# Strassen pairs of the last up projection: the first product is copied between banks by ScalarE and added onto by TensorE, in a new order of the seven products

## The chip, the cores and the metric

One core of one Trainium2 chip. The metric is device time in microseconds, the median of several executions.

## What is computed

Two blocks of a transformer follow each other on a sequence of 512 tokens with 1024 features: sparse attention, a convolutional feed-forward, a state-space mixer, a second feed-forward, and then a block with a short convolution and the gated feed-forward of which the change touches the up projection:

```python
def swiglu(h, w_gate_up, w_down):
    g, u = jnp.split(h @ w_gate_up, 2, axis=-1)
    return (jax.nn.silu(g) * u) @ w_down
...
h = modulate(rms_norm_2(x, norm_gains[i, 2]), sh_f, sc_f)
h = swiglu(h, ffn_w_gate_up[i], ffn_w_down[i])
x = x + g_f[:, None, :] * rms_norm_2(h, norm_gains[i, 3])
```

`w_gate_up` is 1024 x 5632: 22 tiles of 128 gate features and 22 of 128 value ("rise") features. Everything is float32.

## The kernel before, in words

Activations lie with features on the 128 partitions and the 512 tokens along the free dimension, in two halves, HEAD (tokens 0 to 255) and TAIL (256 to 511). Every float32 product is made from three matmuls in a reduced format: each operand is split into a high part (a ScalarE copy to `fp32r`) and a low part (VectorE: the operand less its high part), and TensorE adds hi x hi, hi x lo and lo x hi in a PSUM bank. Weights come in panels of 128 x 1024 by DMAs of SyncE's queue into `raw` buffers (three, and from the pairs on a fourth, `raw_more`); ScalarE writes `whi`, VectorE writes `wlo`, in four slots.

The last up projection, `UP3`, has 44 panels, gate and value tiles alternating. The first 8 (`CLASSIC`) are multiplied in the ordinary way, 24 matmuls of 512 tokens each. The other 36 form 18 pairs (`PAIRS`), one gate and one value tile, and each pair is one step of Strassen's scheme in Winograd's form: the weights of the pair are a 2 x 2 matrix of blocks (A11, A12 the two halves of the gate tile's 1024 inputs, A21, A22 those of the value tile), the activations another, and seven products of 12 matmuls of 256 tokens take the place of eight. The weight sums of the scheme, S1 to S4, are made by GpSimd for each pair in four 512-wide operations (`wsum`, lines 877 to 884); the activation sums (`t_hi`, `t_lo`) are made once.

The weights of a pair are five *units*, each with a high part (`unit_hi`, line 2019) and a low part (`unit_lo`, line 2861): A11 (for P1), S21 (1024 wide, P6 and P5), A12 (P2), S34 (1024 wide, P7 and P3), A22 (P4). A unit's slot is free when the last product that uses it is done; `s_ulo` counts the low parts made, and every product waits for its unit.

Nothing is scheduled automatically. Each engine's order is written by hand: `pairs_up3` for TensorE, one loop over pairs n for ScalarE, one for VectorE, one for GpSimd, and semaphores join them. TensorE takes P1, P6, P5, P7, P2, P4, P3 of pair n and then goes to pair n+1. There are three banks to a pair, X, Y and Z, in two sets that alternate. X gets P1 and then P2 on top (gate head). Y gets P6, P7 and P4 on top of each other, Z gets P5 and P3. ScalarE copies P1 out of X into `first_p` (line 2064), and five VectorE sums of 256 tokens (`part`, line 2874) put the results together, each from a bank and an SBUF tensor:

```python
P(1): part_u[0] = Y(P6) + first_p
P(2): part_u[1] = Y(P6+P7) + first_p
P(3): rise tail = Z(P5) + part_u[1]
P(4): rise head = Y(P6+P7+P4) + first_p
P(5): c12 (gate tail) = Z(P5+P3) + part_u[0]
```

(the five calls of `part`, abridged). Each reads a bank onto which TensorE's next product waits to be added: `s_part` counts them. ScalarE applies silu to the head (from X, line 2038) and the tail (from `c12`, line 2041), and VectorE multiplies all 512 tokens at once (`pair_hidden`, line 2880). VectorE runs, for each n: c12 of pair n-1, low part of S34(n), hidden product of n-1, P(1), low parts of A22(n) and A11(n+1), P(2), P(3), low parts of S21(n+1) and A12(n+1), P(4). In pairs 1 to 4 and in the last one the hidden tiles are split into parts for the down projection as well (`hidden_hi`, line 2030; `hidden_lo`, line 2867), which write over operands no longer in use. The down projection `DOWN3` follows with its panels in three parts.

## Time and profile before

| | us |
|---|---|
| median of 3 runs | 2101.13 |
| lowest, highest | 2096.67, 2101.19 |
| the profiled execution | 2104.0 |
| its span | 2102.3 |
| TensorE busy in it | 2055.5 |
| VectorE busy | 1389.3 |
| ScalarE busy | 906.7 |
| GpSimd busy | 254.7 |

The profiled execution is one run, 2.9 us above the median; its span is shorter than its time by what lies around the program. Busy times include overlap of an instruction's end with the next one's start, so that a full engine shows 100% whatever the spacing of its matmuls; the count of matmuls in a stretch tells more.

### The profile page before, as it was taken

To read this page: it belongs to the slowest core of one execution; us is meant where nothing else is said; L and a number is where in the kernel's file an instruction comes from. 1 tells how busy PE (TensorE), PEld (TensorE's weight loads), DVE (VectorE), ACT (ScalarE), POOL (GpSimd) and SP (SyncE) were. 2 spreads that over 40 slices of the span, in tenths; PEclk is the share of its full clock that TensorE was granted. 3 is DMA by queue.
4 is the path that set the end of the run, shared out by engine and by line. 5 is a ranking of instruction groups with operands and counts; after the bars stand their busy time and mean duration, and the time that the engine had idled before them with its cause. 6 is when DMAs were issued, how large, how long until landed. Compare 5 with 4: busy or idle time off the path is not lost.

```text
span 2102.3 us, 30885 instructions
## 1 busy us (share of the span) xinstructions
PE 2055.5 (98%) x12072; PEld 1737.5 (83%) x12072; DVE 1389.3 (66%) x2383; ACT 906.7 (43%) x1641; POOL 254.7 (12%) x227
## 2 busy tenths in 40 slices
PE   8999999999999999998899999999999999999998
PEld 6877779888888988787789888888898898999887
DVE  5378847877755588537864877766465457888624
ACT  4267754534331354438742543432241234444521
POOL 0000002000000110004601100000020013565101
PEclk9999999999999999999899999999999999999999
DMA  8110002332246323335422232236422322233331
GB/s 276 61 41 22 21 12 81 111 100 91 90 157 233 111 81 104 100 103 164 138 81 81 86 105 100 91 113 234 145 91 91 101 71 73 99 103 109 111 90 61
DMA packets 69696, 217.04 MB, mean 103 GB/s; under 512 B 8112, under 2 KB 11568, under 8 KB 69296
## 3 DMA queue, kind: packets, MB, share of 16 engines
q1 hardware_dynamic: 67536, 208.72, 30.2%
q10 hardware_dynamic: 2016, 6.36, 0.9%
q8 instruction: 96, 1.57, 0.3%
q14 instruction: 48, 0.39, 0.1%
HBM read 211.70 MB, written 2.23 MB: 102 GB/s over the span
## 4 chain that ended last, share of the span: by engine, by line
PE 86%; DVE 8%; ACT 2%; issue 2%; DMA 1%; POOL 1%; SPq 0%; ACTq 0%; DVEq 0%
PE bank L951 23%; PE bank L953 23%; PE bank L952 23%; PE bank L972 3%; PE bank L974 2%; PE bank L973 2%; PE bank L1299 1%; DVE pbuf L2412 1%; PE bank L1276 1%; PE bank L894 1%; DVE pbuf L2431 1%; PE bank L1198 1%; PE bank L1253 1%; POOL h L826 1%; PE bank L925 1%
## 5 line engine op out<-in xcount | busy, mean ns | idle before, releaser
L951 PE MATMUL bank<-xhi,whi 128*128 128x512 f32 (+1 forms) x1624 | 615.6, 379 | 14.9 <-DVE xlo L2124 8.2
L953 PE MATMUL bank<-xhi,wlo 128*128 128x512 f32 (+1 forms) x1624 | 607.5, 374 | 0.0
L952 PE MATMUL bank<-xlo,whi 128*128 128x512 f32 (+1 forms) x1544 | 579.5, 375 | 0.0
L1560 ACT ACTIVATE whi<-raw 128x1024 fp32r<-128x1024 f32 (+1 forms) x283 | 293.0, 1037 | 617.8 <-PE bank L953 592.8
L2110 DVE TENSOR_TENSOR wlo<-raw,whi 128x1024 fp32r<-128x1024 f32 (+1 forms) x283 | 341.5, 1207 | 260.8 <-ACT whi L1560 260.2
L951 PEld LDWEIGHTS bank<-xhi,whi 128*128 128x128 f32 x1624 | 306.9, 189 | 78.6 <-issue 13.0
L953 PEld LDWEIGHTS bank<-xhi,wlo 128*128 128x128 f32 x1624 | 306.8, 189 | 58.1
L952 PEld LDWEIGHTS bank<-xlo,whi 128*128 128x128 f32 x1544 | 292.2, 189 | 53.8
L826 POOL TENSOR_TENSOR h<-tmp,h 128x256 f32<-128x256 f32 x92 | 82.6, 919 | 1475.6 <-DVE tmp L2135 1471.3
L951 PE MATMUL bank<-hid_hi,whi 128*128 128x512 f32 (+1 forms) x416 | 151.3, 364 | 0.0
L953 PE MATMUL bank<-hid_hi,wlo 128*128 128x512 f32 (+1 forms) x416 | 149.8, 360 | 0.0
L952 PE MATMUL bank<-hid_lo,whi 128*128 128x512 f32 (+1 forms) x416 | 149.7, 360 | 0.0
L2278 DVE TENSOR_TENSOR upad<-bank,rstd_b 128x512 f32<-128x512 f32 x88 | 60.6, 690 | 72.7 <-PE bank L953 67.4
L953 PEld LDWEIGHTS bank<-hid_hi,wlo 128*128 128x128 f32 x416 | 78.4, 188 | 12.6
L951 PEld LDWEIGHTS bank<-hid_hi,whi 128*128 128x128 f32 x416 | 78.5, 189 | 12.4
L952 PEld LDWEIGHTS bank<-hid_lo,whi 128*128 128x128 f32 x416 | 78.4, 189 | 12.4
L972 PE MATMUL bank<-t_hi,whi 128*128 128x256 f32 x288 | 82.7, 287 | 2.2 <-DVE part_u L2874 2.1
L1648 ACT ACTIVATE tmp<-upad,par 128x512 f32<-128x512 f32 x88 | 70.6, 805 | 31.8 <-DVE upad L2278 31.8
L974 PE MATMUL bank<-t_hi,wlo 128*128 128x256 f32 x288 | 81.3, 282 | 0.0
L973 PE MATMUL bank<-t_lo,whi 128*128 128x256 f32 x288 | 81.3, 282 | 0.0
L1749 ACT ACTIVATE pbuf<-pbuf,stat 128x512 f32<-128x512 f32 (+3 forms) x128 | 70.3, 552 | 15.9 <-DVE stat L2415 15.9
L952 PE MATMUL bank<-hid_l,whi 128*128 128x512 f32 (+1 forms) x208 | 74.9, 360 | 0.0
(340 smaller groups left out, 3675.2 us busy)
## 6 DMA issues: line engine op xcount, KB each, us to landing
raw<-w SPq DMA_DIRECT2D x286, 512.0 KB, 3.3
ada_w<-w_ada SPq DMA_DIRECT2D x64, 384.0 KB, 4.1
raw<-w SPq DMA_DIRECT2D x24, 384.0 KB, 3.3
row<-cum_rows SPq DMA_DIRECT2D x32, 256.0 KB, 3.6
xbuf<-exp_rows SPq DMA_DIRECT2D x24, 256.0 KB, 3.6
raw_more<-w SPq DMA_DIRECT2D x9, 512.0 KB, 3.2
w_k<-w_cmp ACTq DMA_DIRECT2D x1, 2048.0 KB, 11.4
w_v<-w_cmp ACTq DMA_DIRECT2D x1, 2048.0 KB, 7.7
```

Source lines behind the costliest of these rows:

```text
L826: pool.tensor_tensor(h[:, j, hs], tmp[:, j % 2, hs], h[:, j, hs], ALU.add).then_inc(s_h, 1)
L951: pe.matmul(bk[:, tok], whi[w][:, cols], x_hi, start=k == 0, stop=False, skip_group_check=split)
L952: pe.matmul(bk[:, tok], whi[w][:, cols], x_lo, start=False, stop=False, skip_group_check=split)
L953: return pe.matmul(bk[:, tok], wlo[w][:, cols], x_hi, start=False, stop=last, skip_group_check=split)
L972: pe.matmul(to, whi[w][:, cols], x_hi, start=begins and kb == 0, stop=False, skip_group_check=True)
L973: pe.matmul(to, whi[w][:, cols], x_lo, start=False, stop=False, skip_group_check=True)
L974: mm = pe.matmul(to, wlo[w][:, cols], x_hi, start=False, stop=ends and kb == 3, skip_group_check=True)
L1560: act.activation(whi[g % SLOTS][:, 0:n], raw[RAW_OF[g]][:, 0:n], ACT.Copy).then_inc(s_hi, 1)
L1648: act.activation(tmp[:, c % 2, :], upad[:, c % 2, 2:2 + S], ACT.Identity, scale=col("ffn_w", 3 * k + 2), bias=col("ffn_b", k)).then_inc(s_ ...
L1749: act.activation(pbuf[:, s % 3, g, 0:n], pbuf[:, s % 3, g, 0:n], ACT.Exp, scale=QSCALE, bias=stat[:, b, 4 + g:5 + g], accum_out=stat[:, b, ...
L2110: dve.tensor_tensor(wlo[g % SLOTS][:, 0:n], raw[RAW_OF[g]][:, 0:n], whi[g % SLOTS][:, 0:n].bitcast(F32), ALU.subtract).then_inc(s_lo, 1)
L2278: dve.tensor_tensor(upad[:, c % 2, 2:2 + S], in_bank(c)[:, :], rstd_b[:, :], ALU.mult)\
```

## The change

Bank Y now starts from P1. ScalarE copies bank X to bank Y (`seed`), and TensorE adds P6, P7 and P4 onto it. So Y holds in turn U2 = P1 + P6, U3 = U2 + P7 and the value tile's head, U3 + P4. ScalarE keeps U2 and U3 in SBUF (`keep_u2`, `keep_u3`), VectorE makes the gate tail from Z and U2 (`gate_tail`), the rise tail from Z and U3 (`corner_tail`), and the hidden tile in two halves: the head directly from bank Y (`hidden_head`), the tail from SBUF (`hidden_tail`). TensorE's order is P1(0), and then for each n P5, P6, P2, P7, P1(n+1), P4, P3. The hidden tiles split during the pairs are so in pairs 4 to 7, not 1 to 4. GpSimd's code moves into a function and keeps its order. Helpers get the phase's name as an argument; lines that change for this alone, and the buffers for split hidden tiles that follow the new last uses, are left out here.

```diff
-ORDER_P = ("P1", "P6", "P5", "P7", "P2", "P4", "P3")
-UNIT_LAST = {"A11": "P1", "S21": "P5", "A12": "P2", "S34": "P3", "A22": "P4"}
+UNIT_LAST = {"A11": "P1", "S21": "P6", "A12": "P2", "S34": "P3", "A22": "P4"}
...
+def products_of(name):
+    order = [(0, "P1")]
+    for n in range(PAIRS[name]):
+        order += [(n, p) for p in ("P5", "P6", "P2", "P7")]
+        order += [(n + 1, "P1")] if n + 1 < PAIRS[name] else []
+        order += [(n, "P4"), (n, "P3")]
+    return order
...
             def pairs_up3():
-                for n in range(PAIRS):
-                    if n < 2:
-                        pe.wait_ge(s_ev, EV["UP3"] + (6, 8)[n])
-                    else:
-                        pe.wait_ge(s_sg, SG3 + CLASSIC // 2 + 2 * (n - 2) + 1)
-                    pair_product(n, "P1", "X")
-                    if n >= 2:
-                        pe.wait_ge(s_part, 5 * (n - 2) + 4)
-                    pair_product(n, "P6", "Y")
-                    if n >= 2:
-                        pe.wait_ge(s_part, 5 * (n - 2) + 5)
-                    pair_product(n, "P5", "Z")
-                    pe.wait_ge(s_part, 5 * n + 1)
-                    pair_product(n, "P7", "Y")
-                    pe.wait_ge(s_p1, n + 1)
-                    pair_product(n, "P2", "X")
-                    pe.wait_ge(s_part, 5 * n + 2)
-                    pair_product(n, "P4", "Y")
-                    pe.wait_ge(s_part, 5 * n + 3)
-                    pair_product(n, "P3", "Z")
+                first(0)
+                for n in range(PAIRS["UP3"]):
+                    if n >= 2:
+                        pe.wait_ge(s_c12, pair_made("UP3", n - 2))
+                    pair_product("UP3", n, "P5", "Z")
+                    pe.wait_ge(s_seed, pair_made("UP3", n))
+                    pair_product("UP3", n, "P6", "Y")
+                    pair_product("UP3", n, "P2", "X")
+                    pe.wait_ge(s_u2, pair_made("UP3", n))
+                    pair_product("UP3", n, "P7", "Y")
+                    if n + 1 < PAIRS["UP3"]:
+                        first(n + 1)
+                    pe.wait_ge(s_u3, pair_made("UP3", n))
+                    pair_product("UP3", n, "P4", "Y")
+                    pe.wait_ge(s_c22, pair_made("UP3", n))
+                    pair_product("UP3", n, "P3", "Z")
...
+            def seed(n):
+                act.wait_ge(s_prod, PRODUCT["UP3", n, "P1"])
+                if n < 2:
+                    act.wait_ge(s_ev, EV["UP3"] + (6, 8)[n])
+                else:
+                    act.wait_ge(s_hh, pair_made("UP3", n - 2))
+                act.activation(half_of(pair_bank(n, "Y")), half_of(pair_bank(n, "X")), ACT.Copy).then_inc(s_seed, 1)
+            def keep_u2(n):
+                act.wait_ge(s_prod, PRODUCT["UP3", n, "P6"])
...
+                act.activation(u2[:, n % 2, :], half_of(pair_bank(n, "Y")), ACT.Copy).then_inc(s_u2, 1)
+            def keep_u3(n):
+                act.wait_ge(s_prod, PRODUCT["UP3", n, "P7"])
...
+                act.activation(u3[:, :], half_of(pair_bank(n, "Y")), ACT.Copy).then_inc(s_u3, 1)
...
-            for n in range(PAIRS):
-                unit_hi(n, "S34")
+            seed(0)
+            for n in range(PAIRS["UP3"]):
+                unit_hi("UP3", n, "S34")
                 if n:
                     pair_silu(n - 1, TAIL)
-                act.wait_ge(s_prod, product_done(n, "P1"))
-                if n >= 2:
-                    act.wait_ge(s_part, 5 * (n - 2) + 4)
-                act.activation(first_p[:, n % 2, :], half_of(pair_bank(n, "X")), ACT.Copy).then_inc(s_p1, 1)
-                unit_hi(n, "A22")
-                unit_hi(n + 1, "A11")
-                unit_hi(n + 1, "S21")
-                if 1 <= n < 5:
-                    hidden_hi(n - 1)
-                if n == PAIRS - 1:
+                unit_hi("UP3", n, "A22")
+                unit_hi("UP3", n + 1, "A11")
+                keep_u2(n)
+                unit_hi("UP3", n + 1, "S21")
+                pair_silu(n, HEAD)
+                unit_hi("UP3", n + 1, "A12")
+                if 4 <= n < 8:
+                    hidden_hi(n - 4)
+                if n == PAIRS["UP3"] - 1:
                     for k in range(4, 8):
                         hidden_hi(k)
-                unit_hi(n + 1, "A12")
-                pair_silu(n, HEAD)
+                keep_u3(n)
+                if n + 1 < PAIRS["UP3"]:
+                    seed(n + 1)
...
-            for n in range(PAIRS):
+            for n in range(PAIRS["UP3"]):
                 if n:
-                    part(n - 1, 5, c12[:, :], "Z", "P3", part_u[:, 0, :])
-                unit_lo(n, "S34")
+                    gate_tail(n - 1)
+                unit_lo("UP3", n, "S34")
                 if n:
-                    pair_hidden(n - 1)
-                dve.wait_ge(s_p1, n + 1)
-                part(n, 1, part_u[:, 0, :], "Y", "P6", first_p[:, n % 2, :])
-                unit_lo(n, "A22")
-                unit_lo(n + 1, "A11")
-                if 1 <= n < 5:
-                    hidden_lo(n - 1)
-                part(n, 2, part_u[:, 1, :], "Y", "P7", first_p[:, n % 2, :])
-                dve.wait_ge(s_part, 5 * n + 2)
-                part(n, 3, rise[:, cols_of(TAIL)], "Z", "P5", part_u[:, 1, :])
-                unit_lo(n + 1, "S21")
-                unit_lo(n + 1, "A12")
-                if n == PAIRS - 1:
+                    hidden_tail(n - 1)
+                unit_lo("UP3", n, "A22")
+                unit_lo("UP3", n + 1, "A11")
+                if 4 <= n < 8:
+                    hidden_lo(n - 4)
+                unit_lo("UP3", n + 1, "S21")
+                unit_lo("UP3", n + 1, "A12")
+                if n == PAIRS["UP3"] - 1:
                     for k in range(4, 7):
                         hidden_lo(k)
-                    weight_lo(START["DOWN3"])
-                part(n, 4, rise[:, cols_of(HEAD)], "Y", "P4", first_p[:, n % 2, :])
+                corner_tail(n)
+                hidden_head(n)
+            weight_lo(START["DOWN3"])
             hidden_lo(7)
```

How the orders of two engines read at the same point, a pair of the steady state. On VectorE, before, from `c12` of one pair to the A11 part of the next but one (`wlo_57` is S34's slot, `wlo_58` that of A22, `wlo_59` that of A11 and A12):

```order
L2874 TENSOR_TENSOR c_205<-bank,part_u 128x256 [waits pair_products_made]
L2861 TENSOR_TENSOR wlo_57<-wsum,whi_53 128x1024 [waits pair_units_hi_made]
L2880 TENSOR_TENSOR hid_f_170<-tmp 128x512 [waits pair_parts_added,gates_silu]
L2874 TENSOR_TENSOR part_u<-bank,first_p 128x256 [waits pair_products_made,first_products_kept]
L2861 TENSOR_TENSOR wlo_58<-raw_52,whi_54 128x512 [waits pair_units_hi_made]
L2861 TENSOR_TENSOR wlo_59<-raw_50,whi_55 128x512 [waits pair_units_hi_made]
```

and after the change:

```order
L2931 TENSOR_TENSOR c_205<-bank,u_203 128x256 [waits gates_silu,pair_products_made]
L2917 TENSOR_TENSOR wlo_57<-wsum,whi_53 128x1024 [waits pair_units_hi_made]
L2951 TENSOR_TENSOR hid_f_170<-tmp 128x256 [waits corner_tails_added,gates_silu]
L2917 TENSOR_TENSOR wlo_58<-raw_52,whi_54 128x512 [waits pair_units_hi_made]
L2917 TENSOR_TENSOR wlo_59<-raw_50,whi_55 128x512 [waits pair_units_hi_made]
```

The units keep their order; the hidden product is half as wide, and the sum between it and A22 is gone. On TensorE, before, where P1 (`whi_55`, `wlo_59`) begins, it follows P3 of the pair ahead:

```order
L972 MATMUL bank<-xhi,whi_53 128x256
L973 MATMUL bank<-xlo,whi_53 128x256
L974 MATMUL bank<-xhi,wlo_57 128x256
L972 MATMUL bank<-xhi,whi_55 128x256 [waits pair_units_lo_made,gates_silu]
L973 MATMUL bank<-xlo,whi_55 128x256
L974 MATMUL bank<-xhi,wlo_59 128x256
```

and now it follows P7 (which reads `t_hi`, `t_lo`) of it:

```order
L996 MATMUL bank<-t_hi,whi_53 128x256
L998 MATMUL bank<-t_lo,whi_53 128x256
L999 MATMUL bank<-t_hi,wlo_57 128x256
L996 MATMUL bank<-xhi,whi_55 128x256 [waits pair_units_lo_made,gates_silu]
L998 MATMUL bank<-xlo,whi_55 128x256
L999 MATMUL bank<-xhi,wlo_59 128x256
```

P1 of the next pair has moved ahead of P4 and P3 of this one, with its wait for the unit's low part. On ScalarE, after the change, from S34's high part on:

```order
L2048 ACTIVATE whi_53<-wsum 128x1024 [waits pair_products_made,weight_sums_made]
L2074 ACTIVATE tmp<-c_205 128x256 [waits hidden_made,gate_tails_added]
L2048 ACTIVATE whi_54<-raw_more 128x512 [waits pair_products_made,raw_landed3]
L2048 ACTIVATE whi_55<-raw_51 128x512 [waits pair_products_made,raw_landed1]
L2090 ACTIVATE u_203<-bank 128x256 [waits gate_tails_added,pair_products_made]
L2048 ACTIVATE whi_56<-wsum 128x1024 [waits pair_products_made,weight_sums_made]
L2070 ACTIVATE tmp<-bank 128x256 [waits hidden_heads_made,pair_products_made]
L2048 ACTIVATE whi_55<-raw_51 128x512 [waits pair_products_made,raw_landed1]
L2097 ACTIVATE u_204<-bank 128x256 [waits corner_tails_added,pair_products_made]
L2083 ACTIVATE bank<-bank 128x256 [waits hidden_heads_made,pair_products_made]
```

In the place of one copy (`first_p`, before A22's high part) stand three: U2 ahead of S21's high part, U3 and the seed of the next pair at the end.

## Rows read from the trace of the kernel before

**Rows 1.** The page, busy time, share of the span and count of instructions

```profile
PE 2055.5 (98%) x12072; PEld 1737.5 (83%) x12072; DVE 1389.3 (66%) x2383; ACT 906.7 (43%) x1641; POOL 254.7 (12%) x227
```

**Rows 2.** Windows of the pair stage: length, busy of PE, PEld, DVE, ACT, POOL, PEclk, DMA

```profile
1800.00:1840.00 40.00, 38.13 (x314) 37.31 (x313) 34.23 (x45) 19.49 (x33) 23.89 (x16) 1.00 0.27 93
1840.00:1965.00 125.00, 125.00 (x1038) 124.19 (x1037) 105.64 (x138) 59.40 (x102) 69.60 (x45) 1.00 0.31 101
```

**Rows 3.** Waits of PE, 1740 to 2000: us in total, times, longest

```profile
PE bank L972 <- DVE part_u L2874: 2.1, 4, 0.9
```

**Rows 4.** Timeline of PE, first matmul, the 61st, first of DOWN3: start, us, engine

```profile
1781.15 0.28 PE L972 MATMUL bank<-xhi,whi 128*128 128x256 f32 x1
...
1788.26 0.28 PE L972 MATMUL bank<-t_hi,whi 128*128 128x256 f32 x1
...
1966.25 0.47 PE L951 MATMUL bank<-xhi,whi 128*128 128x512 f32 x1
```

**Rows 5.** Timeline of PE and DVE around one wait and around a pair's end

```profile
1798.21 0.41 DVE L2874 TENSOR_TENSOR part_u<-bank,first_p 128x256 f32<-128x256 f32 x1
...
1798.68 0.39 PE L972 MATMUL bank<-t_hi,whi 128*128 128x256 f32 x1 [0.29 <-DVE part_u L2874]
...
1798.91 0.28 PE L973 MATMUL bank<-t_lo,whi 128*128 128x256 f32 x1
...
1801.67 0.28 PE L972 MATMUL bank<-xhi,whi 128*128 128x256 f32 x1
...
1801.87 0.42 DVE L2874 TENSOR_TENSOR c<-bank,part_u 128x256 f32<-128x256 f32 x1 [0.71 <-PE bank L974]
```

**Rows 6.** Timeline of DVE (VectorE) over one pair, steady state

```profile
1872.50 1.22 DVE L2861 TENSOR_TENSOR wlo<-wsum,whi 128x1024 fp32r<-128x1024 f32 x1
...
1875.33 0.42 DVE L2874 TENSOR_TENSOR c<-bank,part_u 128x256 f32<-128x256 f32 x1 [0.68 <-PE bank L974]
1876.48 1.44 DVE L2861 TENSOR_TENSOR wlo<-wsum,whi 128x1024 fp32r<-128x1024 f32 x1 [0.73 <-ACT whi L2019]
1877.85 0.68 DVE L2880 TENSOR_TENSOR hid_f<-tmp 128x512 f32<-128x512 f32 x1
1878.45 0.41 DVE L2874 TENSOR_TENSOR part_u<-bank,first_p 128x256 f32<-128x256 f32 x1
1878.79 1.44 DVE L2861 TENSOR_TENSOR wlo<-raw_more,whi 128x512 fp32r<-128x512 f32 x1
1880.15 1.78 DVE L2861 TENSOR_TENSOR wlo<-raw,whi 128x512 fp32r<-128x512 f32 x1
```

**Rows 7.** Timeline of POOL (GpSimd) in the same pair

```profile
1873.88 1.58 POOL L877 TENSOR_TENSOR wsum<-raw 128x512 f32<-128x512 f32 x1 [2.65 <-DVE wlo L2861]
1875.55 1.30 POOL L879 TENSOR_TENSOR wsum<-wsum,raw 128x512 f32<-128x512 f32 x1
1878.01 1.67 POOL L882 TENSOR_TENSOR wsum<-raw,raw 128x512 f32<-128x512 f32 x1 [1.16 <-DVE wlo L2861]
1879.64 1.74 POOL L884 TENSOR_TENSOR wsum<-raw,wsum 128x512 f32<-128x512 f32 x1
```

**Rows 8.** Timeline of ACT (ScalarE) in the same pair

```profile
1875.39 1.06 ACT L2019 ACTIVATE whi<-wsum 128x1024 fp32r<-128x1024 f32 x1 [2.11 <-PE bank L974]
1876.36 0.40 ACT L2041 ACTIVATE tmp<-c 128x256 f32<-128x256 f32 x1
1876.75 0.39 ACT L2064 ACTIVATE first_p<-bank 128x256 f32<-128x256 f32 x1
```

**Rows 9.** Timeline of ACT and DVE in the last pair

```profile
1959.34 1.15 ACT L2030 ACTIVATE t_hi<-hid_f 128x512 fp32r<-128x512 f32 x2 [0.57 <-PE bank L974]
...
1964.92 1.23 DVE L2110 TENSOR_TENSOR wlo<-raw,whi 128x1024 fp32r<-128x1024 f32 x1
```

**Rows 10.** Windows of PE at an earlier tail: length, busy, PEclk, DMA

```profile
1532.00:1536.00 4.00, 3.01 (x22) 0.90 0.00 0
1536.00:1540.00 4.00, 4.00 (x26) 0.68 0.40 131
```

More of the change, by code:

```diff
@@ L91 @@
 TOTAL = len(PANELS)
-CLASSIC = 8
-PAIR0 = START["UP3"] + CLASSIC
-PAIRS = (TILES["UP3"] - CLASSIC) // 2
-PAIRED = range(PAIR0, PAIR0 + 2 * PAIRS)
-GATE, RISE = 0, 1
-ORDER_P = ("P1", "P6", "P5", "P7", "P2", "P4", "P3")
+CLASSIC = {"UP3": 8}
+PAIR0 = {name: START[name] + c for name, c in CLASSIC.items()}
+PAIRS = {name: (TILES[name] - c) // 2 for name, c in CLASSIC.items()}
+PAIRED = {PAIR0[name] + g: (name, g // 2, g % 2) for name in CLASSIC for g in range(2 * PAIRS[name])}
+PAIRS_BEFORE, _n = {}, 0
@@ L113, in unit_made @@
-def unit_made(n, name):
-    return 5 * n + UNITS.index(name) + 1
-def slot_of(place):
-    return (PAIR0 + place) % SLOTS
+def products_of(name):
[5 more added lines that the diff above has]
+    return order
+PRODUCT = {(_name, *_np): 7 * PAIRS_BEFORE[_name] + _k + 1
+           for _name in CLASSIC for _k, _np in enumerate(products_of(_name))}
@@ L123, in made, with pair_made, unit_made, sums_done @@
+def pair_made(name, n):
+    return PAIRS_BEFORE[name] + n + 1
+def unit_made(name, n, unit):
+    return 5 * (PAIRS_BEFORE[name] + n) + UNITS.index(unit) + 1
+def sums_done(name, n, k):
+    return 4 * (PAIRS_BEFORE[name] + n) + k
+def slot_of(name, place):
+    return (PAIR0[name] + place) % SLOTS
 def made(g):
-    return g + 1 if g < PAIR0 else g + 1 - len(PAIRED)
+    return sum(1 for k in range(g + 1) if k not in PAIRED)
 RAW_OF, RAW_NTH, RAW_BEFORE = {}, {}, {}
-_held, _uses = {}, [0] * (RAWS + 1)
+_held, _uses, _k, _base = {}, [0] * (RAWS + 1), -1, 0
@@ L441, in build @@
         raw.append(sb("raw_more", [P, D], F32, at(120)))
-        first_p = sb("first_p", [P, 2, S // 2], F32, at(124))
-        part_u = sb("part_u", [P, 2, S // 2], F32, at(126))
+        u2 = sb("u2", [P, 2, S // 2], F32, at(124))
+        u3 = sb("u3", [P, S // 2], F32, at(126))
         c12 = sb("c12", [P, S // 2], F32, at(128))
@@ L832, in _, with weight_sums @@
                 add_update(name, TAIL)
+            def weight_sums(name):
+                for n in range(PAIRS[name]):
+                    gate = PAIR0[name] + 2 * n
+                    a1, a2 = raw[RAW_OF[gate]], raw[RAW_OF[gate + 1]]
+                    s2, s1, s3, s4 = (wsum[:, k, :] for k in range(4))
+                    for g in (gate, gate + 1):
+                        pool.wait_ge(s_raw[RAW_OF[g]], 16 * (RAW_NTH[g] + 1))
+                    if n:
+                        pool.wait_ge(s_ulo, unit_made(name, n - 1, "S21"))
+                    pool.tensor_tensor(s1, a2[:, 0:S], a2[:, S:2 * S], ALU.add).then_inc(s_wsum, 1)
+                    pool.wait_ge(s_wsum, sums_done(name, n, 1))
+                    pool.tensor_tensor(s2, s1, a1[:, 0:S], ALU.subtract).then_inc(s_wsum, 1)
+                    if n:
+                        pool.wait_ge(s_ulo, unit_made(name, n - 1, "S34"))
+                    pool.tensor_tensor(s3, a1[:, 0:S], a2[:, 0:S], ALU.subtract).then_inc(s_wsum, 1)
+                    pool.wait_ge(s_wsum, sums_done(name, n, 2))
+                    pool.tensor_tensor(s4, a1[:, S:2 * S], s2, ALU.subtract).then_inc(s_wsum, 1)
             def decay_state(G):
@@ L866, in _ @@
                 add_update(name, TAIL)
[L868 to L884 removed]
+            weight_sums("UP3")
             add_update("DOWN3", HEAD)
@@ L1038, in project_in @@
                     lead(TAIL, (3,))
-                for t in range(first, CLASSIC if name == "UP3" else TILES[name]):
+                for t in range(first, CLASSIC.get(name, TILES[name])):
                     for (tile, _), extra in between:
@@ L2923, in _ @@
                     for k in range(4, 7):
                         hidden_lo(k)
[L2925 to L2926 removed]
+                corner_tail(n)
+                hidden_head(n)
+            weight_lo(START["DOWN3"])
             hidden_lo(7)
+            gate_tail(PAIRS["UP3"] - 1)
             hidden_lo(8)
[L2929 removed]
             weight_lo(START["DOWN3"] + 1)
```

207 lines of the change are left out of this document (106 added, 101 removed).

## The prediction

> **What bounds the kernel now.** I read the page's busy shares first, then the windows over the last up projection, the waits of TensorE there, and the timelines of one pair engine by engine. TensorE is busy for 98% of the span [rows 1]. In the pair stage it is busy for all of the 125 us from 1840 to 1965, at the full granted clock; in the 40 us before that it is idle for 1.9 us [rows 2]. The waits say whom it waits for: VectorE's sums of products, four times, the longest 0.9 us [rows 3]. So outside the first few pairs, the stage can't become shorter except by fewer or denser matmuls, and the change alters neither.
>
> The stage starts at 1781.15 and the down projection's first matmul at 1966.25 [rows 4]: **185.1 us** for 18 pairs of 84 matmuls. The first 60 of them take 1788.26 - 1781.15 = 7.11 us [rows 4], 0.1185 us each; the mean of the undisturbed windows is 125 / 1038 = 0.1204 us [rows 2]. I take 0.119, so a product of 12 matmuls is 1.43 us and 126 products are 180.2 us. What waits cost now, small ones included, is 185.1 - 180.2 = 4.9 us. That is all that a perfect change could give.
>
> **What sets VectorE's time in a pair.** The reader should look at the low parts that VectorE makes from raw or wsum. The 1024-wide one takes 1.22 us at 1872.50 and 1.44 us at 1876.48; the 512-wide ones take 1.44 and 1.78 us at 1878.79 and 1880.15 [rows 6], against 0.68 us for the 512-wide hidden product at 1877.85. Put GpSimd's four weight sums beside them [rows 7] and the ends interlock. GpSimd's second sum ends at 1876.85 and VectorE's S34 part 1.07 us later, at 1877.92. The hidden product ends at 1878.53, GpSimd's third sum 1.15 us later at 1879.68, VectorE's A22 part 0.55 us later at 1880.23, GpSimd's fourth sum 1.15 us later at 1881.38, VectorE's A11 part 0.55 us later at 1881.93. They take strict turns: operations of the two engines that read two SBUF tensors are not running together, and the row's duration includes the turn of the other. The small sums that read one PSUM bank and one SBUF tensor stay at 0.41 to 0.42 us amid this.
>
> From the gate sum c12 at 1875.33, the moment at which the last product of a pair is seen, to the A11 part of the next pair is therefore 1881.93 - 1875.33 = **6.60 us**. Today this costs nothing, because P1 of the next pair, which needs it, comes after seven products, 10.0 us.
>
> **The change, by parts.**
>
> 1. *TensorE's order.* P1 of pair n+1 now stands before P4 and P3 of pair n, behind P5, P6, P2, P7: it is due 4 x 1.43 = 5.72 us after P5 begins, not 10.0. P5 of the next pair begins 0.20 us before c12's sum starts (1801.67 and 1801.87) [rows 5].
>
> 2. *VectorE's chain to the A11 part, after the change*, counted from the gate sum. ScalarE's high part of S34 starts 0.06 us and VectorE's low part 1.15 us after it, as now [rows 6, 8]. It then runs unhindered in 1.22 us, since GpSimd's first two sums now come earlier against it (they follow S21's low part at 7.2 and are over near 10.2, before the next gate sum at 10.8): 2.37. The hidden product is halved to 256 columns; 1024 to 512 wide saves 0.54 us (1.22 to 0.68), so half of that again: 0.68 - 0.27 = 0.41, ending at 2.29 + 0.41 = 2.70. Then the turns, with their measured 1.15, 0.55, 1.15, 0.55: 3.85, 4.40, 5.55, **6.10**. That the sum part_u of 0.41 us between them is gone gives nothing, since it ran in GpSimd's turn.
>
> 3. *The new wait.* A stopped TensorE resumes 0.17 us after its releaser: the sum ends at 1798.62, the second matmul comes at 1798.91, which puts the first at an effective 1798.79 [rows 5]. P1 of pair n+1 so starts at 0.20 + 6.10 + 0.17 = 6.47 and is due at 5.72: a stall of 0.75 us in each pair. The circle closes over P4 and P3 (S34's slot is free only when P3 of the pair is done): 6.47 + 3 x 1.43 = **10.76 us a pair**, against 84 x 0.1204 = 10.11 now [rows 2].
>
> 4. *Copies by ScalarE.* The seed from bank to bank has no row. From below, 0.39 us as first_p's copy from bank to SBUF; from above 1.06 us, the longest copy of this engine in the stage [rows 8]. P1 is over at 7.9 and P6 is due at 12.2, so even 1.06 is hidden three times over; I take 0.39. u2 has only P2 as cover: ScalarE sees a product's end 0.06 us after VectorE does (1875.39 and 1875.33) [rows 6, 8], 0.26 us after the next could begin; with 0.39 and 0.17 that is 0.82 of 1.43 us. At 1.06 us it would be 1.49, 0.06 too late, and that would be taken out of the 0.75 us stall that follows. u3 and the corner sum have the stalled P1 and P4 as cover. Cost: 0. If the 0.75 went away, u2 would be next, with 0.6 us to spare.
>
> 5. *VectorE and its waits.* One sum of five and half a product less, 0.7 us a pair; TensorE's four waits for part_u go [rows 3], with the slow resuming around them a good part of the 4.9 us. That is already counted, as the new stage is built from 1.43 us products.
>
> 6. *The end.* In the last pair four copies of hidden tiles stand ahead of u3 on ScalarE, and no P1 covers it. After P2: 0.26, silu 0.3, four copies of 0.53 (1.15 us for two that overlap by 0.1) [rows 9], copy 0.39, 0.17: 3.2 us against P7's 1.43: a stall of 1.8. VectorE's low part of the first down panel now stands behind the last hidden_head, so after P4: 0.20 + 0.34 + 1.23 [rows 9] + 0.17 = 1.94 against P3's 1.43: 0.5 us.
>
> **Sum.** First five products 7.15 (the first pair has no earlier gate sum or hidden product ahead of its A22 and A11 parts, so I give P1 of the second no stall), sixteen circles 16 x 10.76 = 172.2, nine products at the end 12.9, 1.8 and 0.5: 194.5 us against 185.1. That is **+9.4 us** on the profiled execution, 2104.0 to 2113.4 us. The median of the runs shown is 2101.13, so I forecast **2110.5 us**. What this kernel's measurement can tell from no change is 0.3%, 6.3 us.
>
> The page TensorE: Matmul & The Clock Gate of the Trainium skill, section Back-to-back issue gap, gives N/2.4 + 2.5 ns between isolated full-speed matmuls, 109 ns for 256 columns. By it a product would be 1.31 us and the new circle 6.47 + 3.93 = 10.4 us; the rows show 119 ns, weight loads included, and the sum goes by them.
>
> **Bounds of this case.** If GpSimd's third sum does not wait for the hidden product, 0.33 us a pair goes: 2105. If the second sum still delays S34's part by 0.22 us and the two waits ahead of P4 and P3 cost 0.1 us each although satisfied, 0.42 us a pair comes: 2117. (0.77)
>
> **Rival one, not slower: TensorE stays the bound.** Place: GpSimd's third sum. Were the A22 part to get its turn before that sum, not after it, A22 would end near 3.25, the sum at 4.40 and the A11 part at 4.95, and P1 could start at 5.32, before it is due. It decides at 0.75 us: anything that brings the A11 part that much forward ends the stall. The time is 180.2 + 2.3 = 182.5 us for the stage, 2.6 less: **2098.5**. For it: the order of requests is near, GpSimd asks about 0.1 to 0.2 us after S34's part ends, and VectorE's A22 part can ask from 0.3 us on. Against it: at both handovers in rows 6 and 7 the engine that waited longer went next. (0.15)
>
> **Rival two: the clock.** After a gap ahead of the tail matmuls the granted clock fell to 0.90 and 0.68 in two 4 us windows at 1532 to 1540 [rows 10], 4 x 0.10 + 4 x 0.32 = 1.7 us lost. Were each new stall to bring that, 16 x 1.7 = 27 us come on top: **2138**. Against it: the 1.9 us of idle time in 1800 to 1840 lie in stalls of this same kind, once a pair, at a granted clock of 1.00 [rows 2]. The Trainium skill, same page, section A second HAM failure mode: psum-queue depth-cycling, says frequent short idle spells between groups of matmuls make the clock swing; the windows beside the present stalls do not show it. (0.04)
>
> **Rival three: ScalarE late.** If its copies out of a bank took 1.5 us, u2 would be 0.26 + 1.5 + 0.17 = 1.93 us after P6, 0.5 us past P2, and u3 would come late as well: about 0.5 us a pair in place of, not on top of, part of the 0.75 us, so 2106 to 2115. Against it: no copy of this size in rows 8 is above 0.40 us. (0.04)
>
> **Numbers.** The likeliest case holds 2105 to 2117. To leave out no more than 2 in 10 the range must take in rival one: **2098 to 2117**. Slower by over 0.3% (above 2107.4): the first case without its lowest edge (0.72), rival two (0.04) and half of three (0.02), 0.78. Within 0.3%: that edge (0.05), most of rival one (0.13) and a little of three (0.01), 0.19. Faster: what is left of both, 0.03, since all waits together are only 4.9 us.
>
> **What would show it.** Right: TensorE's first matmul of P1 (bank from xhi) idle 0.5 to 0.8 us before it in each pair, released by VectorE's wlo; a pair's period of 10.7 to 10.9 us; GpSimd's rows alternating with VectorE's as now; no wait for the seed or u2; VectorE's busy share of the stage down although the stage is longer; one wait of over 1 us before the last P4. Wrong: a period near 10.0 (rival one), windows below 1.00 in the stage (rival two), or waits that end on ScalarE's u or bank copies in most pairs.

## The result and the profile after

| | before | after |
|---|---|---|
| median of 6 runs each, us | 2099.12 | 2111.06 |
| lowest, highest | 2095.93, 2101.19 | 2106.68, 2113.28 |
| the profiled execution, its span | 2104.0, 2102.3 | 2109.76, 2108.0 |
| pair stage in the profile (first pair matmul to first of the down projection) | 185.1 | 194.9 |

The ratio is 1.0057, with an interval of 1.0046 to 1.0068: **slower by 9.7 to 14.3 us**. The forecast was 9.4 us more, to 2110.5. The profiled execution of the kernel before is none of its six runs; that of the changed kernel is one of its own.

The page's busy shares, as in [rows 1]:

```profile
PE 2049.9 (97%) x12072; PEld 1730.0 (82%) x12072; DVE 1373.6 (65%) x2347; ACT 918.0 (44%) x1677; POOL 250.4 (12%) x227
```

TensorE is busy for less time in a longer span, and VectorE for less too: 1373.6 us against 1389.3. Less busy time in a longer program. The windows of the pair stage (columns as in [rows 2]):

```profile
1796.00:1836.00 40.00, 38.19 (x319) 37.68 (x318) 28.89 (x36) 20.47 (x38) 21.28 (x16) 1.00 0.28 94
1836.00:1957.00 121.00, 114.06 (x940) 111.95 (x938) 90.63 (x104) 62.61 (x117) 65.09 (x46) 1.00 0.30 97
```

Where before 125 us held 1038 matmuls without a gap [rows 2], 121 us now hold 940: one in 0.1287 us, not 0.1204, at the same granted clock of 1.00. The waits of TensorE from 1740 to 2000, to set beside [rows 3]:

```profile
PE bank L996 <- DVE wlo L2917: 9.6, 16, 0.6
PE bank L996 <- ACT u L2097: 1.4, 1, 1.4
```

The waits for part_u are gone. In their place stand sixteen for a low part of weights, and one of 1.4 us for `u`. The timeline of TensorE at one of the sixteen:

```profile
1880.75 0.28 PE L999 MATMUL bank<-t_hi,wlo 128*128 128x256 f32 x1
1881.63 0.36 PE L996 MATMUL bank<-xhi,whi 128*128 128x256 f32 x1 [0.60 <-DVE wlo L2917]
1881.82 0.28 PE L998 MATMUL bank<-xlo,whi 128*128 128x256 f32 x1
```

The row at 1880.75 is the last matmul of P7, the one at 1881.63 the first of P1 of the next pair. Normal spacing is 0.12 us; this one takes 0.88, so P7 and the gap behind it take 2.18 us in place of 1.42. The product that is stopped takes 1.50 itself, as its first two matmuls lie 0.19 us apart. Together one stall costs 0.84 us. VectorE in the same pair, from the gate sum on, to set beside [rows 6]:

```profile
1875.37 0.42 DVE L2931 TENSOR_TENSOR c<-bank,u 128x256 f32<-128x256 f32 x1 [1.00 <-PE bank L999]
1876.53 1.22 DVE L2917 TENSOR_TENSOR wlo<-wsum,whi 128x1024 fp32r<-128x1024 f32 x1 [0.73 <-ACT whi L2048]
1877.67 0.42 DVE L2951 TENSOR_TENSOR hid_f<-tmp 128x256 f32<-128x256 f32 x1
1878.00 1.78 DVE L2917 TENSOR_TENSOR wlo<-raw_more,whi 128x512 fp32r<-128x512 f32 x1
1879.71 1.77 DVE L2917 TENSOR_TENSOR wlo<-raw,whi 128x512 fp32r<-128x512 f32 x1
1881.40 1.21 DVE L2917 TENSOR_TENSOR wlo<-wsum,whi 128x1024 fp32r<-128x1024 f32 x1
...
1883.14 0.41 DVE L2938 TENSOR_TENSOR tmp<-bank,u 128x256 f32<-128x256 f32 x1
```

and GpSimd, beside [rows 7]:

```profile
1873.76 1.28 POOL L867 TENSOR_TENSOR wsum<-wsum,raw 128x512 f32<-128x512 f32 x1
1877.83 1.41 POOL L870 TENSOR_TENSOR wsum<-raw,raw 128x512 f32<-128x512 f32 x1 [2.78 <-DVE wlo L2917]
1879.20 1.73 POOL L872 TENSOR_TENSOR wsum<-raw,wsum 128x512 f32<-128x512 f32 x1
1883.10 1.28 POOL L865 TENSOR_TENSOR wsum<-raw_more 128x512 f32<-128x512 f32 x1 [2.17 <-DMA raw_more<-w]
```

S34's part now takes 1.22 us, unhindered, since GpSimd's second sum was over at 1875.04, ahead of the gate sum at 1875.37. The hidden product is half as wide and ends at 1878.09. From there the turns run as they ran before: GpSimd's third sum ends at 1879.24 (1.15 later), the A22 part at 1879.78 (0.54), GpSimd's fourth at 1880.93 (1.15), the A11 part at 1881.48 (0.55), and TensorE starts right behind it. Each of the two parts takes 1.78 us for 0.55 us of work. The A11 part is there 6.11 us after the gate sum, 0.49 us earlier than before (6.60). Counted from the start of the pair's P5, which is 0.20 us earlier, that is 6.31, and there P1 now wants it at 5.7, not at 10.0. The last row of VectorE, a sum of a bank and an SBUF tensor, takes 0.41 us although GpSimd's sum at 1883.10 runs beside it in 1.28 us, as long as the unhindered one at 1873.76.

ScalarE in the same pair (its high part of S34, the copies U2 and U3, and the seed):

```profile
1875.43 1.06 ACT L2048 ACTIVATE whi<-wsum 128x1024 fp32r<-128x1024 f32 x1 [2.54 <-PE bank L999]
...
1878.22 0.38 ACT L2090 ACTIVATE u<-bank 128x256 f32<-128x256 f32 x1 [0.38 <-PE bank L999]
...
1881.06 0.38 ACT L2097 ACTIVATE u<-bank 128x256 f32<-128x256 f32 x1 [0.51 <-PE bank L999]
1883.33 0.37 ACT L2083 ACTIVATE bank<-bank 128x256 f32<-128x256 f32 x1 [1.89 <-PE bank L999]
```

The seed from bank to bank takes 0.37 us (all 18 of them 368 ns), less than the 0.39 of first_p's copy [rows 8]. At 1883.33 it is far ahead of P6 of the next pair.

The last pair, ScalarE (silu, four copies of hidden tiles, U3) and then TensorE:

```profile
1966.09 0.38 ACT L2070 ACTIVATE tmp<-bank 128x256 f32<-128x256 f32 x1 [1.04 <-PE bank L999]
1966.37 1.14 ACT L2059 ACTIVATE xhi<-hid_f 128x512 fp32r<-128x512 f32 x2
1967.41 1.14 ACT L2059 ACTIVATE xlo<-hid_f 128x512 fp32r<-128x512 f32 x2
1968.45 0.37 ACT L2097 ACTIVATE u<-bank 128x256 f32<-128x256 f32 x1
```

```profile
1968.87 0.38 PE L996 MATMUL bank<-t_hi,whi 128*128 128x256 f32 x1 [1.40 <-ACT u L2097]
...
1972.25 0.47 PE L976 MATMUL bank<-xhi,whi 128*128 128x512 f32 x1 [0.28 <-issue]
```

U3's copy at 1968.45 waits behind the four copies that begin at 1966.37; the first matmul of P4 behind it starts at 1968.87 after 1.40 us of idle time. The profile puts the 0.28 us of idle time ahead of the down projection down to issue; the low part of its first panel, which it also needs, ends at 1972.15:

```profile
1970.93 1.22 DVE L2167 TENSOR_TENSOR wlo<-raw,whi 128x1024 fp32r<-128x1024 f32 x1
```

### The profile page after: what moved, and what is told of

It reads as the page before. It is cut to its first block, busy times and chain, and to the rows that moved or that the text cites. A ratio compares the mean times of both kernels' runs of the same rounds, so it can differ in the third digit from the quotient of the medians.

```text
span 2108.0 us, 30938 instructions
## 1 busy us (share of the span) xinstructions
PE 2049.9 (97%) x12072; PEld 1730.0 (82%) x12072; DVE 1373.6 (65%) x2347; ACT 918.0 (44%) x1677; POOL 250.4 (12%) x227
## 3 DMA queue, kind: packets, MB, share of 16 engines
q10 hardware_dynamic: 2016, 6.36, 0.9%
## 4 chain that ended last, share of the span: by engine, by line
PE 84%; DVE 10%; ACT 3%; issue 2%; POOL 0%; DMA 0%; SPq 0%; ACTq 0%; DVEq 0%
PE bank L976 24%; PE bank L977 23%; PE bank L978 23%; DVE wlo L2917 3%; PE bank L996 2%; PE bank L999 1%; PE bank L998 1%; PE bank L1327 1%; DVE pbuf L2469 1%; PE bank L919 1%; PE bank L1304 1%; ACT whi L2048 1%; DVE pbuf L2488 1%; PE bank L1226 1%; PE bank L1281 1%
## 5 line engine op out<-in xcount | busy, mean ns | idle before, releaser
L1590 ACT ACTIVATE whi<-raw 128x1024 fp32r<-128x1024 f32 (+1 forms) x283 | 293.1, 1038 | 619.0 <-PE bank L978 593.9
L978 PEld LDWEIGHTS bank<-hid_hi,wlo 128*128 128x128 f32 x416 | 78.4, 188 | 12.7
## 6 DMA issues: line engine op xcount, KB each, us to landing
w_k<-w_cmp ACTq DMA_DIRECT2D x1, 2048.0 KB, 10.8
```

The lines of the kernel that those rows point to most:

```text
L978: return pe.matmul(bk[:, tok], wlo[w][:, cols], x_hi, start=False, stop=last, skip_group_check=split)
L1590: act.activation(whi[g % SLOTS][:, 0:n], raw[RAW_OF[g]][:, 0:n], ACT.Copy).then_inc(s_hi, 1)
```

## The experiments

Ten kernels in all are compared by two numbers of their traces: the stage, as above, and the period, the mean over six pairs in its middle (the ninth to the fourteenth). Both are counted between first matmuls of products, twelve matmuls each. These hardly depend on what else happens in the program. Whole times are to be compared with those of the kernel before on the same chip: its median was 2100.64 beside e1 to e4 and 2097.85 beside e5 to e8. A whole time of one run is only a rough check.

| | stage, us | period, us | whole time, us |
|---|---|---|---|
| before | 185.1 | 10.15 | 2099.12 (median of 6) |
| the change | 194.9 | 10.80 | 2111.06 (median of 6) |
| e1 hidden product behind A11's part | 185.0 | 10.05 | 2098.1 (median), ratio to before 0.9987 (0.9977 to 0.9997) |
| e2 A11's parts first | 195.8 | 10.73 | 2108.4 (one run) |
| e3 GpSimd's last two sums cut | 182.7 | 9.97 | 2098.1 (one run) |
| e4 seed three times | 195.6 | 10.80 | 2108.8 (one run) |
| e5 before, with P1 early | 197.8 | 11.07 | 2108.3 (one run) |
| e6 P1 one product later | 194.4 | 10.72 | 2105.3 (one run) |
| e7 last pair reordered | 192.8 | 10.81 | 2106.8 (one run) |
| e8 all moves | 179.5 | 9.97 | 2093.73 (median), ratio to before 0.9981 (0.9970 to 0.9992) |

The theories under test. **Turns**: an operation of VectorE with two SBUF inputs and one of GpSimd with two run one after the other; this puts the A11 part at 6.1 us after the gate sum, and the new order wants it sooner. **Volume**: VectorE has too much queued, and each duration is its own. **Copies**: ScalarE's seed, U2 and U3 set the period.

### e1: the hidden product behind A11's part

```diff
                 unit_lo("UP3", n, "S34")
-                if n:
-                    hidden_tail(n - 1)
                 unit_lo("UP3", n, "A22")
                 unit_lo("UP3", n + 1, "A11")
+                if n:
+                    hidden_tail(n - 1)
```

> One move in the changed kernel: VectorE's hidden product of the tail (0.42 us) goes behind the low parts of A22 and A11 instead of ahead of them. Theory 'turns' (VectorE and GpSimd alternate on operations with two SBUF inputs, and P1 is now due early): A22's part now asks before GpSimd's third sum and gets the first turn, so the A11 part comes 1.15 + 0.3 us earlier, P1's wait is gone, the period falls from 10.81 to 10.0 us, the stage from 194.9 to about 185 (3 us of waits ahead of P3 and 1.5 ahead of the last P4 stay), the time to that of the kernel before, ratio 0.998 to 1.002. Theory 'volume' (VectorE has simply too much queued ahead, each row's duration is its own): 0.33 us earlier, period 10.45, stage 189.5. Theory 'copies' (ScalarE's seed, U2 and U3 set the period): no change, 10.8.

Measured: period 10.05, stage 185.0. VectorE from S34's part on, and GpSimd's third and fourth sum:

```profile
1873.35 1.22 DVE L2917 TENSOR_TENSOR wlo<-wsum,whi 128x1024 fp32r<-128x1024 f32 x1 [0.73 <-ACT whi L2048]
1874.50 0.68 DVE L2917 TENSOR_TENSOR wlo<-raw_more,whi 128x512 fp32r<-128x512 f32 x1
1875.10 1.79 DVE L2917 TENSOR_TENSOR wlo<-raw,whi 128x512 fp32r<-128x512 f32 x1
1876.81 1.51 DVE L2951 TENSOR_TENSOR hid_f<-tmp 128x256 f32<-128x256 f32 x1
```

```profile
1874.66 1.68 POOL L870 TENSOR_TENSOR wsum<-raw,raw 128x512 f32<-128x512 f32 x1 [2.06 <-DVE wlo L2917]
1876.30 1.73 POOL L872 TENSOR_TENSOR wsum<-raw,wsum 128x512 f32<-128x512 f32 x1
```

A22's part asks at 1874.50, GpSimd's third sum at 1874.66: VectorE is first, and its part takes 0.68 us in place of 1.78. The A11 part ends at 1876.89, 3.54 us after S34's part began; in the changed kernel it was 4.95 (1876.53 to 1881.48). So moving 0.42 us of work away gave 1.41 us. This is what Volume can't explain, since it allows 0.33 to 0.42. It can't be Copies either, as ScalarE's order is untouched. The hidden product itself now pays a turn, 1.51 us at 1876.81, and no wait of TensorE comes of it. The waits left in the stage:

```profile
PE bank L996 <- ACT u L2097: 1.4, 1, 1.4
PE bank L996 <- DVE tmp L2938: 1.3, 4, 0.4
```

These are the corner sum in the four pairs that split hidden tiles, and the end. The stage and the whole time are back at those of the kernel before. The median is even a trifle under it (2098.1 against 2100.64), by 0.13%, and the stages (185.0 and 185.1) do not show where that would come from. The period is not quite steady: from the eleventh pair on a product takes 1.44 us, in the two pairs before it 1.42 to 1.43.

### e2: A11's parts ahead of A22's

```diff
-                unit_hi("UP3", n, "A22")
                 unit_hi("UP3", n + 1, "A11")
+                unit_hi("UP3", n, "A22")
...
-                unit_lo("UP3", n, "A22")
                 unit_lo("UP3", n + 1, "A11")
+                unit_lo("UP3", n, "A22")
```

(and the counts of the units made, to match)

> In the changed kernel the high and low parts of A11 of the next pair are made ahead of those of A22, on ScalarE and VectorE. 'Turns': P1's wait is gone (its part comes 1.7 us earlier), but A22's part is now behind two of GpSimd's turns and so is the load that waits for it; its panel lands later, GpSimd's first two sums shift into S34's part, and the waits move to P4 and, by the corner sum, to P3: period 10.6 to 10.8, stage 194. 'Volume': the A11 part is 0.6 to 1.7 us earlier with nothing in its place, period 10.0 to 10.2, stage 184 to 187. 'Copies': 10.8 with the wait still ahead of P1.

Measured: period 10.73, stage 195.8, no better than the change, and 1.8 us longer than the 194 expected. The wait for A11 is gone, and others have come, the longest in the first pair that splits hidden tiles:

```profile
PE bank L1001 <- DVE tmp L2943: 6.4, 14, 1.6
```

The releaser is the corner sum (tmp), ahead of P3. How the shift works its way round is in VectorE's rows (S34, A11, A22) and in GpSimd's first two sums:

```profile
1875.02 2.08 DVE L2922 TENSOR_TENSOR wlo<-wsum,whi 128x1024 fp32r<-128x1024 f32 x1 [0.73 <-ACT whi L2053]
...
1877.35 1.77 DVE L2922 TENSOR_TENSOR wlo<-raw,whi 128x512 fp32r<-128x512 f32 x1
1879.05 1.77 DVE L2922 TENSOR_TENSOR wlo<-raw_more,whi 128x512 fp32r<-128x512 f32 x1
```

```profile
1873.36 1.29 POOL L870 TENSOR_TENSOR wsum<-raw 128x512 f32<-128x512 f32 x1 [3.90 <-DMA raw<-w]
1874.72 1.29 POOL L872 TENSOR_TENSOR wsum<-wsum,raw 128x512 f32<-128x512 f32 x1
```

GpSimd's first sum starts at 1873.36, behind the landing of its panel (3.90 us of idle time put down to the DMA), the second at 1874.72, and it is in the way of S34's part, which takes 2.08 us, not 1.22. The panel came late because its load waits for A22's part, which is now the last of the turns. In the pair before these rows A22's part ended at 1870.01, and SyncE's queue issued the load right behind it:

```profile
1870.03 2.06 SPq L731 DMA_DIRECT2D raw<-w  x2
```

The period and the way of the delay came out as Turns had them, and against Volume's 10.0 to 10.2. It also shows that to bring A11 forward is not enough: someone must lose the turn who can afford it. In e1 that is the hidden product, here it was A22.

### e3: GpSimd's third and fourth sum cut to 8 columns

```diff
+                    m = 8 if n else S
-                    pool.tensor_tensor(s3, a1[:, 0:S], a2[:, 0:S], ALU.subtract).then_inc(s_wsum, 1)
+                    pool.tensor_tensor(s3[:, 0:m], a1[:, 0:m], a2[:, 0:m], ALU.subtract).then_inc(s_wsum, 1)
                     pool.wait_ge(s_wsum, sums_done(name, n, 2))
-                    pool.tensor_tensor(s4, a1[:, S:2 * S], s2, ALU.subtract).then_inc(s_wsum, 1)
+                    pool.tensor_tensor(s4[:, 0:m], a1[:, S:S + m], s2[:, 0:m], ALU.subtract).then_inc(s_wsum, 1)
```

> Leaves out computation: from the second pair on GpSimd makes 8 of 512 columns of its third and fourth weight sum, everything else of the changed kernel stays. 'Turns': VectorE's A22 and A11 parts fall from 1.78 to about 0.7 us, P1 is not late, period 10.0, stage 183.5. 'Volume' and 'copies': period 10.8, parts of 1.78 us as before.

This leaves out 504 of 512 columns of both sums, so the kernel computes something else.

Measured: period 9.97, stage 182.7, 0.8 us under the 183.5 expected. VectorE's A22 and A11 parts:

```profile
1873.07 0.69 DVE L2918 TENSOR_TENSOR wlo<-raw_more,whi 128x512 fp32r<-128x512 f32 x1
1873.68 0.69 DVE L2918 TENSOR_TENSOR wlo<-raw,whi 128x512 fp32r<-128x512 f32 x1
```

0.69 us each against 1.78 and 1.77. VectorE's and ScalarE's programs are untouched here, and so is TensorE's; all that was taken away is GpSimd's share of the turns, 2 x 1.15 us, and with it the whole stall. Volume and Copies both wanted 10.8.

### e4: the seed three times

```diff
+                for k in range(2):
+                    act.activation(half_of(pair_bank(n, "Y")), half_of(pair_bank(n, "X")), ACT.Copy).then_inc(s_more, 1)
+                    act.wait_ge(s_more, 2 * n + k + 1)
                 act.activation(half_of(pair_bank(n, "Y")), half_of(pair_bank(n, "X")), ACT.Copy).then_inc(s_seed, 1)
```

> In the changed kernel ScalarE makes the copy from bank X to bank Y three times in a row, each waiting for the one before (about 0.4 us more each, 0.8 us in all). 'Turns' and 'volume': hidden by the products P4, P3 and P5, period 10.8, stage 195 to 195.5. 'Copies': the period grows by up to 0.8 us, stage up to 209.

Measured: period 10.80, stage 195.6 (0.7 more, a hair over the 195 to 195.5 expected; most of it lies in the products of the first pair, where only P5 lies between P1 and P6 and the copies stand at the head of ScalarE's queue), and the same sixteen waits:

```profile
PE bank L997 <- DVE wlo L2921: 9.6, 16, 0.6
```

The copy could be three times as long at no cost in the steady state (in the stage as a whole 0.7 us). That clears the seed. U2 and U3 are not touched here; that the copies as a whole don't set the period is shown by e1 and e3, which leave ScalarE's program as it is and end the stall.

### e5: the kernel before, with P1 early

```diff
                     pair_product(n, "P2", "X")
+                    if n + 1 < PAIRS:
+                        first(n + 1)
                     pe.wait_ge(s_part, 5 * n + 2)
                     pair_product(n, "P4", "Y")
```

(`first` holds P1 with its wait, taken from the head of the loop; the counts of products match)

> The kernel before with one thing of the change: P1 of pair n+1 stands between P2 and P4 of pair n, and nothing of the copies between banks. 'Turns': P1 is due 5.7 us after a pair's begin and its part is there at 6.6 + 0.4; the VectorE sum that P7 waits for comes before it in the same queue, so part of the wait shows ahead of P7 and part ahead of P1; period 11.0 to 11.3, stage 197 to 200, 12 to 15 us above the kernel before. 'Copies' (that the new copies are to blame and the order is harmless): period 10.1, stage 185.

Measured: period 11.07, stage 197.8, 12.7 us above the kernel before.

```profile
PE bank L981 <- DVE part_u L2888: 9.5, 17, 0.6
```

VectorE in one pair, the sum that P7 waits for and the A22 and A11 parts (one row for both):

```profile
1864.89 0.42 DVE L2888 TENSOR_TENSOR part_u<-bank,first_p 128x256 f32<-128x256 f32 x1
1865.22 3.13 DVE L2875 TENSOR_TENSOR wlo<-raw,whi 128x512 fp32r<-128x512 f32 x2
```

One half of the change, the early P1, in the old kernel makes the stage longer by more than the whole change does (12.7 us against 9.8): the order is what costs. That the rest of the change takes part of it back by making VectorE's chain shorter is the reading of this difference, not a test of it. Nearly all of the wait is at P7, whose sum part_u stands on VectorE ahead of the A22 and A11 parts, behind S34's part and the hidden product. It ends at 1865.31, and P7, which now comes two products after the pair's begin, not three, was due at 1864.64. This wait comes from VectorE's queue and not from a turn, as S34's part (1.23 us) and the hidden product (0.68 us) ran unhindered. It doesn't set the period, though. The A11 part ends at 1868.35, behind two of GpSimd's turns, and P1 starts another 0.2 us late behind it. That closes the circle: 0.20 to the gate sum, 6.36 to the A11 part, 0.22 to resume and three products give 11.06. That the wait is shared like this was expected in kind; that nearly all is at P7 I had not put in numbers.

### e6: P1 one product later

```diff
-                    if n + 1 < PAIRS["UP3"]:
-                        first(n + 1)
                     pe.wait_ge(s_u3, pair_made("UP3", n))
                     pair_product("UP3", n, "P4", "Y")
+                    if n + 1 < PAIRS["UP3"]:
+                        first(n + 1)
```

> The changed kernel with P1 of the next pair one product later, behind P4 and ahead of P3. The A11 part is then in time (there 6.47 us after a pair's begin, due at 7.9). 'Turns' with the dependences as they are: the cover of U3's copy is gone, so P4 starts 0.26 + 0.38 + 0.17 = 0.8 us after P7's end and the period is 7 x 1.42 + 0.8 = 10.8 again, now with all of the wait ahead of P4 and on ScalarE; stage 195 to 196. If the wait for A11 were not one of place, it would stay ahead of P1.

Measured: period 10.72, stage 194.4, a little under the 195 to 196 that was expected. P4's first matmul comes 0.64 us late and P4 itself takes 1.52 us, which makes 0.74 us, not 0.8.

```profile
PE bank L997 <- ACT u L2098: 9.4, 18, 1.4
```

Eighteen waits for U3 on ScalarE and none for weights. So P1 stood where it did as the cover of U3's copy, and the change's order had two constraints that collide: U3 needs a product behind P7, and the only free one needs A11.

### e7: the last pair

```diff
+                    if n == PAIRS["UP3"] - 1:
+                        pe.wait_ge(s_seed, pair_made("UP3", n))
+                        pair_product("UP3", n, "P6", "Y")
+                        pe.wait_ge(s_c12, pair_made("UP3", n - 2))
+                        pair_product("UP3", n, "P5", "Z")
+                        pe.wait_ge(s_u2, pair_made("UP3", n))
+                        pair_product("UP3", n, "P7", "Y")
+                        pair_product("UP3", n, "P2", "X")
...
                 keep_u2(n)
+                if n == PAIRS["UP3"] - 1:
+                    keep_u3(n)
...
                 if n == PAIRS["UP3"] - 1:
+                    weight_hi(START["DOWN3"])
                     for k in range(4, 8):
                         hidden_hi(k)
...
+                corner_tail(n)
                 if n == PAIRS["UP3"] - 1:
+                    weight_lo(START["DOWN3"])
                     for k in range(4, 7):
                         hidden_lo(k)
-                corner_tail(n)
                 hidden_head(n)
```

> The changed kernel with its last pair alone done otherwise: products in the order P6, P5, P7, P2, P4, P3, U3's copy ahead of silu and of the four copies of hidden tiles, the down projection's first low part ahead of the last hidden head. The steady state is untouched, period 10.8. The three long products at the end (2.98, 1.52 and 1.86 us where 1.42 is undisturbed) fall to 1.42 to 1.6: stage 192.8 to 193.3, 1.6 to 2.1 us under the changed kernel's 194.9.

Measured: stage 192.8, 2.1 us less, period 10.81. No product behind the last pair's P1 takes over 1.46 us.

```profile
PE bank L996 <- DVE wlo L2932: 9.6, 16, 0.6
PE bank L976 <- DVE hid_l L2937: 0.3, 1, 0.3
```

The sixteen waits for wlo stay, that for `u` is gone; a new small one of 0.3 us, for a part of a hidden tile, lies in the down projection.

### e8: all moves together

The edits of e1 and e7, and the splits of hidden tiles in pairs 4 to 7 moved behind the seed and the hidden head:

```diff
-                if 4 <= n < 8:
-                    hidden_hi(n - 4)
...
                     seed(n + 1)
+                if 4 <= n < 8:
+                    hidden_hi(n - 4)
...
-                if 4 <= n < 8:
-                    hidden_lo(n - 4)
...
                 hidden_head(n)
+                if 4 <= n < 8:
+                    hidden_lo(n - 4)
```

> The changed kernel with the hidden product behind A11's part, the last pair as in the run before, and the splits of hidden tiles in pairs 4 to 7 behind the seed on ScalarE and behind the hidden head on VectorE. 'Turns': no wait over 0.15 us left in the stage, period 10.0, stage 180.5 to 182, 3 to 4.5 us under the kernel before's 185.1: ratio 0.9975 to 0.999. That is the whole of what waits cost there.

Measured: stage 179.5, period 9.97, ratio to the kernel before 0.9981 (0.9970 to 0.9992), so 1.7 to 6.3 us faster (medians 2093.73 and 2097.85 on the same chip). The windows (columns as in [rows 2]) and the waits:

```profile
1796.00:1836.00 40.00, 40.00 (x339) 40.00 (x338) 32.26 (x38) 22.66 (x42) 25.14 (x17) 1.00 0.31 107
1836.00:1950.00 114.00, 114.00 (x963) 114.00 (x962) 91.51 (x107) 62.77 (x116) 68.17 (x44) 1.00 0.31 106
```

```profile
PE bank L976 <- DVE hid_l L2937: 0.3, 1, 0.3
```

963 matmuls in 114 us, 0.1184 each, and no wait left in the stage, which is 5.6 us shorter than before. This is 1 us better than the 180.5 to 182 expected. It is the one version that beats both kernels in the stage by more than a fraction of a microsecond without leaving anything out; in the whole time it is 0.2% faster than the kernel before. The change's idea holds once VectorE's order is put right, but not all of the gain is its own: 3.6 of the 5.6 us lie in pairs 1 to 4 of the kernel before, which split hidden tiles there and take 10.56 to 11.45 us for 9.97 in e8. Whether the old order of products would gain as much with its splits moved was not tested.

## Why the prediction was right

*TensorE's order and the new wait (items 1 to 3).* Held, step by step. S34's part unhindered: 1.22 us, as given. Hidden product 0.42 us, given 0.41. Turns of 1.15, 0.54, 1.15, 0.55 us, given 1.15, 0.55, 1.15, 0.55. The A11 part 6.11 us after the gate sum, given 6.10. The period 10.80, given 10.76. The missing 0.04 is in the resuming: the A11 part ends at 1881.48, the second matmul of P1 is at 1881.82, which puts the first at an effective 1881.70, 0.22 us behind it, not 0.17. The stall so costs 0.84 us, given 0.75; the rest of that difference is that a product takes 1.42 to 1.43 us and not a full 1.43.

*Copies (item 4).* Cost nothing, as given; the seed was 0.37 us for an estimated 0.39, and e4 shows that three of them in a row, 1.1 us or about the upper bound of 1.06, are hidden from the second pair on. U2 was there at 1878.60, and P7, which waits for it, began at 1879.44 (eleven spacings of 0.119 ahead of 1880.75).

*VectorE's relief (item 5).* The waits for part_u went, and with them the late resuming around them. Sixteen stalls of 0.84 us and 2.1 us at the end make 15.5 us, yet the stage grew by 9.8: some 5.6 us of small waits of the old stage are gone, for 4.9 given. VectorE's busy share in the undisturbed window fell from 85% (105.64 of 125 us) to 75% (90.63 of 121).

*The end (item 6).* P7 and its stall took 2.98 us, so 1.56 of stall against 1.8 given; P3 with the wait behind it 1.86, so 0.44 against 0.5. e7 gives both back, 2.1 us.

*The sum.* The stage 194.9 us against 194.5 given; 9.8 us more than before, 9.4 given. The terms are each a little off and in part make up for each other: the stalls cost 13.4 us more, given 12.0, the end 2.1, given 2.3, and 5.6 came back, given 4.9. That the median of 2111.06 lies so near the forecast of 2110.5 is luck beyond this. The forecast stood on a median before of 2101.13, which six runs put at 2099.12, and the rise was 11.9 us, not 9.4.

*Rival one (TensorE stays the bound)* did not occur, but e1 shows that its mechanism is real and how near it lay: with the hidden product out of the way, A22's part gets its turn first (1874.50 against 1874.66) and the stall is gone. That its time is 2098.1 us, where this rival said 2098.5, is chance: its stage is 185.0 us, where the rival said 182.5. The rival left out the waits ahead of P3 in the four pairs that split hidden tiles, 0.55 to 0.63 us a pair, which the changed kernel hides behind its stall, and it took 1.43 us for products that there take 1.44 from the eleventh pair on. *Rival two (clock)*: 1.00 in all windows of the stage, with a stall of 0.76 us in each pair; no swing of the kind that the Trainium skill (TensorE: Matmul & The Clock Gate, section A second HAM failure mode: psum-queue depth-cycling) describes. *Rival three*: no copy of a bank to SBUF took over 0.39 us, and no wait in the middle of the stage ends on ScalarE.

What stays open: the median rose by 11.9 us, the stage by 9.8. The interval's lower end is 9.7, so the two don't contradict each other, but some 2 us are not placed. In the profiled executions the span outside the stage goes the other way (2102.3 - 185.1 = 1917.2 before, 2108.0 - 194.9 = 1913.1 after). Over the ten kernels it lies between 1908.8 (e5) and 1917.2 with next to no edit there, so single executions can't settle 2 us.

## What to carry to other kernels

When work is moved to an earlier place on the bound engine, look up when each of its inputs is ready now, not only who makes them: slack of 3 us in the old order was what hid the turns of VectorE and GpSimd, and the new order spent it. Where two engines alternate, the order of requests can be worth more than the amount of work, as here: 0.42 us moved out of the way gave 1.41 us in each pair, while 15.7 us less busy time of VectorE in the whole program (1389.3 to 1373.6) did not keep the stage from growing by 9.8 us. And a release that is made late (a slot, a buffer) comes back a pair later through the load that waits for it, as in e2.
